# Two attention layers: the forget-attention groups placed between projections, and x loaded after the modulation blocks

## The chip, the cores and the metric

One core of one Trainium2 chip runs one program. The metric is the device time of that program in microseconds (us), the median of several runs. TensorE (PE) multiplies, VectorE (DVE) and ScalarE (ACT) work on what it leaves in the eight PSUM banks, GpSimd (POOL) does a little, and SyncE (SP) issues the DMA transfers that bring the weights.

## What is computed

A block of 256 tokens of width 1024 goes through two "hybrid" attention layers, then through two mixer layers, a dense SwiGLU and a mixture of experts. Only the attention layers are touched. One of them, cut down:

```python
shift, scale, gate = split(c @ w_ada + b_ada, 3)          # modulation, one row
u = x * (1 + scale) + shift
h = split_cols(u @ w_in)                                  # all projections
o_dsa = dsa_mixer(rope(dq), rope(dk), dv, rope(iq), rope(ik), iw)   # top-64 keys of an indexer
o_fox = fox_mixer(fq, fk, fv, log_sigmoid(f + b_f))       # forget attention, 6 heads, no rope
kc, vc = nsa_compress(h.kc, ...), nsa_compress(h.vc, ...) # silu(blocks @ w1) @ w2
o_nsa = g0*cmp(nq, kc, vc) + g1*slc(rope(nq), rope(ks), vs) + g2*win(rope(nq), rope(kw), vw)
y = (concat(o_dsa, o_fox, o_nsa) * silu(h.gate)) @ w_out
x = layer_norm(alpha * x + (1 + gate) * y)
```

Everything is 32-bit floating point.

## The kernel before

The kernel is written engine by engine: each engine has its own instruction list in program order, and the lists meet only at semaphores. `plan_first` gives every result that TensorE leaves (a "job", such as `nq01` or `S3`) one of eight PSUM banks and a turn in it. `take` makes TensorE wait until the bank is free, `filled` makes a reader wait until it is full, `copied` waits until a job's readers are done. So the order of the work is the order in which the lists are written by hand.

Weights come as "parts" of up to 2 MB through a ring of five slots; the list `loads` sets their order, and a slot is refilled when the last job of `LAST_USE` that reads it is complete. `W_IN_PARTS` cuts `w_in` into these parts. Until the first answer of TensorE is there, SyncE issues the four parts `ada0` to `ada3` of the modulation, with x between `ada1` and `ada2`, and then `idx_q`.

At the start TensorE makes the four modulation rows (`ada_row`, `ada_column`; VectorE sums four of the eight slices of each) and turns x (`turn_x`: 16 transposes into the banks `xT0` to `xT3`). VectorE (`xT0`, `xT2`) and ScalarE (`xT1`, `xT3`) scale and shift these into `uT`. Each of the four jobs holds two of the eight slices `k` that a projection sums over. The first projection, `iq`, waits for all four.

One layer then goes on TensorE in this order: index, DSA and fox projections with the eight `index_scores` between them; the NSA projections `nq01`, `nq2`, `kcvc`, `ks`, `vsw` (values), `kwg`; the compression (`ch`: 32 matmuls with 30 columns, line 979; `ckv`); then 20 attention groups (`GROUPS`): five "fox" (n = 0 to 4), two "cmp", five "win", five "slc", three "dsa". `rotate` makes the rotated copy that VectorE's `rope` needs, `ada_gate` the broadcast of the output gate from a sum that VectorE makes in the slots of `ada4` and `ada5` (`ada_sum`, eight steps each). A group is a chain over three engines:

- TensorE `scores(n)` (line 1035), VectorE `row_max(n)` (line 2265), ScalarE exponentials (line 1684),
- TensorE `transposes(n)` (line 1078), VectorE `copy_pT(n)` (line 2282),
- TensorE `outputs(n)` (line 1099), VectorE `mixed(n)` (line 2311).

The group loop runs them staggered: `scores(n)`, `transposes(n - 1)`, `outputs(n - 2)`. The projection of the output gate (1024 columns) is cut into eight `gate_part` pieces (line 991, about 3.6 us each at full clock) and strewn between the groups by `GATE_PART_AT`; ScalarE copies them out by `GATE_COPY_AT`, and VectorE's top-64 search (`select`, 16 steps) is strewn by `SELECT_AT`. `scores(0)` waits for everything the groups need, `ckv` and all ropes among it, although a fox group needs only fox projections.

Of the kernel before, what the change touches and what calls it, by code (L numbers as in the profile page):

```python
# [8 lines left out]
P = 128  # L9
D = 1024  # L10
T = 256
NT = T // P
KD = D // P
# [24 lines left out]
for _n, _w in _names:  # L38
# [5 lines left out]
              ("nsa_q", "nsa_q"), ("nsa_kc", "nsa_ks"), ("nsa_vs", "nsa_g")]  # L44
# [175 lines left out]
def plan_first(jobs, l):  # L220
# [34 lines left out]
    add("ckv", 3, 2)  # L255
    for k in range(NG + 2):
        if k < NG:
            add(f"S{k}", [0, 1, 7][k % 3])
        if 1 <= k <= NG:
            add(f"T{k - 1}", [2, 3][(k - 1) % 2])  # L260
        if k >= 2:
            add(f"O{k - 2}", [4, 5][(k - 2) % 2])
# [82 lines left out]
def build(nc, A, out_dram):  # L345
# [35 lines left out]
    for l in range(DEPTH):  # L381
        for a, b in W_IN_PARTS:
# [6 lines left out]
            if a == "nsa_kc":  # L389
                add_load((l, "cmp_w1"), 2 * CMP_LEN // 2, HD, A["cmp_w1"][l].rearrange("v (j p) m -> p (v j) m", p=P))  # L390
# [20 lines left out]
    with ctx:  # L411
# [68 lines left out]
        relu, rope_t1 = p_sb, pT  # L480
# [169 lines left out]
        def _(sp):  # L650
# [21 lines left out]
            for n, (name, k, width, src) in enumerate(loads):  # L672
# [7 lines left out]
                if name == (0, "ada1"):  # L680
                    sp.dma_start(x[:, :, :], A["x"][0].rearrange("(i p) d -> p i d", p=P)).then_inc(S("x_loaded"), 16)
# [67 lines left out]
        def _(pe):  # L749
# [103 lines left out]
            for q in range(4):  # L853
                if q == 2:
                    turn_x()
# [3 lines left out]
            ada_column(3)  # L859
            for l in range(DEPTH):  # L860
                first, second = slice(0, P), slice(P, T)
                if l == 0:
                    for m in range(4):
                        copied(pe, jobs[0, f"xT{m}"])
                    feats(l, "iq", ("idx_q", 0, P), ("idx_q", P, P))
# [85 lines left out]
                feats(l, "nq01", ("nsa_q", 0, P), ("nsa_q", P, P))  # L951
                ada_gate(0)
                feats(l, "nq2", ("nsa_q", 2 * P, P))
                feats(l, "kcvc", ("nsa_kc", 0, P), ("nsa_vc", 0, P))
                rotate(l, "nq01")
                feats(l, "ks", ("nsa_ks", 0, P))
                rotate(l, "nq2")
                j = jobs[l, "vsw"]
                b = take(pe, j)
                for i in range(NT):  # L960
                    for m, name in enumerate(("nsa_vs", "nsa_vw")):
                        last = tok(b, l, "nsa_vs", at(name), P, i, (2 * i + m) * P)
                done(last, j)
                ada_gate(1)
                j = jobs[l, "kwg"]
                b = take(pe, j)
                feat(b, l, "nsa_kw", 0, P, 0)
                for i in range(NT):
                    last = tok(b, l, "nsa_vs", at("nsa_g"), 18, i, T + 18 * i)
                done(last, j)  # L970
                rotate(l, "ks")

                j = jobs[l, "ch"]
                b = take(pe, j)
                w1 = weights(pe, (l, "cmp_w1"))
                copied(pe, jobs[l, "kcvc"])
                for v in range(2):
                    for t in range(CMP_LEN // 2):
                        last = mm(b[0:HD, 30 * v:30 * v + 30], w1[:, CMP_LEN // 2 * v + t, :], blk[:, v, t, :, :],
                                  start=(t == 0), stop=(t == CMP_LEN // 2 - 1))  # L980
                done(last, j)
                rotate(l, "kw")
# [1756 lines left out]
```

## Time and profile before

| | us |
|---|---|
| median of 3 runs | 2196.99 (2193.92 to 2197.11) |
| the profiled execution | 2193.05 |
| its span in the profile | 2191.0 |
| TensorE busy in it | 2113.2 (96%) |
| VectorE busy | 1504.8 (69%) |
| ScalarE busy | 1003.5 (46%) |

The span is what the records of the profile cover; the 2 us around it are start and end of the program. In the records a matmul on 32-bit data shows as two records, and its end is modelled, so "busy" does not mean full speed. The first 560 us or so of the span are the two attention layers, layer 0 up to about 305 us.

### The profile page before, as it was taken

To read this page: it belongs to the slowest core of one execution; us is meant where nothing else is said; L and a number is where in the kernel's file an instruction comes from. 1 tells how busy PE (TensorE), PEld (TensorE's weight loads), DVE (VectorE), ACT (ScalarE), POOL (GpSimd) and SP (SyncE) were. 2 spreads that over 40 slices of the span, in tenths; PEclk is the share of its full clock that TensorE was granted. 3 is DMA by queue.
4 is the path that set the end of the run, shared out by engine and by line. 5 is a ranking of instruction groups with operands and counts; after the bars stand their busy time and mean duration, and the time that the engine had idled before them with its cause. 6 is when DMAs were issued, how large, how long until landed. Compare 5 with 4: busy or idle time off the path is not lost.

```text
span 2191.0 us, 27918 instructions
## 1 busy us (share of the span) xinstructions
PE 2113.2 (96%) x10564; PEld 1676.5 (77%) x10564; DVE 1504.8 (69%) x1822; ACT 1003.5 (46%) x1074; POOL 52.4 (2%) x56
## 2 busy tenths in 40 slices
PE   7999999999998899999988999999999999999996
PEld 3786666765887599888757888888888888888885
DVE  4454433544398645438858888888898888889886
ACT  1111312122131434313235776777676776777674
POOL 0000000000002000000300000000000000000000
PEclk9997999889999999999998999999999999999998
DMA  9752133611531255453117999999899999999890
GB/s 352 272 186 96 43 125 116 222 39 39 177 99 51 83 174 192 166 183 117 39 56 295 395 374 350 345 352 373 321 376 330 367 347 350 370 326 377 322 354 20
DMA packets 238693, 502.18 MB, mean 229 GB/s; under 512 B 11258, under 2 KB 53010, under 8 KB 238610
## 3 DMA queue, kind: packets, MB, share of 16 engines
q1 hardware_dynamic: 238610, 501.03, 63.9%
q8 instruction: 57, 0.93, 0.2%
q14 instruction: 26, 0.21, 0.0%
HBM read 499.96 MB, written 1.05 MB: 229 GB/s over the span
## 4 chain that ended last, share of the span: by engine, by line
PE 89%; DVE 7%; ACT 2%; issue 2%; DMA 0%; SPq 0%; DVEq 0%; ACTq 0%
PE bank L1469 12%; PE bank L1452 9%; PE bank L1454 9%; PE bank L1453 9%; PE bank L760 6%; PE bank L1162 6%; PE bank L1035 3%; PE bank L991 3%; PE bank L768 3%; PE bank L1132 3%; PE bank L1399 2%; PE bank L1138 2%; PE bank L1369 2%; PE bank L1370 2%; PE bank L1368 2%; PE bank L1334 2%
## 5 line engine op out<-in xcount | busy, mean ns | idle before, releaser
L2560 DVE TENSOR_TENSOR ring_r<-ring,his 128x2048 fp32r<-128x2048 f32 x240 | 549.2, 2291 | 83.5 <-ACT his L1565 83.4
L1565 ACT ACTIVATE his<-ring 128x2048 fp32r<-128x2048 f32 x240 | 460.1, 1918 | 131.1 <-PE bank L1454 77.7
L1452 PE MATMUL bank<-his,xe_hi 128*128 128x512 f32 x896 | 356.0, 397 | 0.2 <-DVE ring_r L2560 0.2
L1454 PE MATMUL bank<-his,xe_lo 128*128 128x512 f32 x896 | 349.4, 390 | 0.0
L1453 PE MATMUL bank<-ring_r,xe_hi 128*128 128x512 f32 x704 | 274.0, 389 | 0.0
L2560 DVE TENSOR_TENSOR more_raw_r<-more_raw,his 128x2048 fp32r<-128x2048 f32 x96 | 219.8, 2291 | 32.1 <-ACT his L1565 32.0
L1565 ACT ACTIVATE his<-more_raw 128x2048 fp32r<-128x2048 f32 x96 | 184.1, 1918 | 57.4 <-PE bank L1469 32.0
L1452 PEld LDWEIGHTS bank<-his,xe_hi 128*128 128x128 f32 x896 | 168.3, 188 | 36.1 <-issue 1.7
L1454 PEld LDWEIGHTS bank<-his,xe_lo 128*128 128x128 f32 x896 | 168.2, 188 | 35.8
L1453 PEld LDWEIGHTS bank<-ring_r,xe_hi 128*128 128x128 f32 x704 | 132.3, 188 | 28.3 <-issue 1.7
L760 PE MATMUL bank<-uT,ring 128*128 128x256 f32 (+4 forms) x704 | 149.9, 372 | 2.7 <-DVE uT L2125 2.7
L1162 PE MATMUL bank<-uT,ring 128*128 128x256 f32 (+1 forms) x768 | 149.9, 357 | 0.0
L760 PEld LDWEIGHTS bank<-uT,ring 128*128 128x128 f32 (+3 forms) x704 | 119.2, 185 | 34.2 <-issue 11.7
L1469 PE MATMUL bank<-his,he_hi 128*128 128x512 f32 x448 | 142.3, 399 | 1.9 <-DVE he_lo L2648 1.9
L1162 PEld LDWEIGHTS bank<-uT,ring 128*128 128x128 f32 x768 | 131.2, 199 | 15.5 <-issue 0.5
L1469 PE MATMUL bank<-his,he_lo 128*128 128x512 f32 x448 | 138.5, 390 | 0.0
L2384 DVE SCALAR_TENSOR_TENSOR cacc<-hpad,cvec,cacc 128x256 f32<-128x256 f32 x240 | 109.6, 529 | 0.1
L1368 PE MATMUL bank<-uT_r,ff_hi 128*128 128x256 f32 (+1 forms) x384 | 108.6, 283 | 0.0
L1370 PE MATMUL bank<-uT_r,ring_r 128*128 128x256 f32 (+1 forms) x384 | 108.2, 282 | 0.0
L1369 PE MATMUL bank<-u_lo,ff_hi 128*128 128x256 f32 (+1 forms) x384 | 108.2, 282 | 0.0
L2081 DVE TENSOR_TENSOR ring_r<-ring,ff_hi 128x2048 fp32r<-128x2048 f32 (+1 forms) x34 | 74.2, 2226 | 49.4 <-ACT ff_hi L1565 49.4
L1469 PEld LDWEIGHTS bank<-his,he_hi 128*128 128x128 f32 x448 | 83.8, 189 | 22.1 <-issue 3.4
(425 smaller groups left out, 3067.5 us busy)
## 6 DMA issues: line engine op xcount, KB each, us to landing
ring<-in_moe_w_gate_dram SPq DMA_DIRECT2D x96, 1024.0 KB, 5.2
ring<-in_moe_w_up_dram SPq DMA_DIRECT2D x80, 1024.0 KB, 5.4
ring<-in_moe_w_down_dram SPq DMA_DIRECT2D x64, 1024.0 KB, 4.9
more_raw<-in_moe_w_down_dram SPq DMA_DIRECT2D x48, 1024.0 KB, 5.0
ring<-in_w_in_dram SPq DMA_DIRECT2D x16, 2048.0 KB, 9.4
more_raw<-in_moe_w_up_dram SPq DMA_DIRECT2D x32, 1024.0 KB, 5.3
ring<-in_w_ada_dram SPq DMA_DIRECT2D x12, 2048.0 KB, 9.3
ring<-in_w_out_dram SPq DMA_DIRECT2D x8, 2048.0 KB, 9.4
```

Source lines behind the costliest of these rows:

```text
L760: last = mm(b[0:n, to + tokens.start:to + tokens.stop], w[:, k, a:a + n], uT[:, k, tokens], start=(k == 0), stop=(k == KD - 1))
L1162: last = mm(b[:, f * T + tokens.start:f * T + tokens.stop], w[:, k, a:a + P], uT[:, k, tokens], start=(k == 0), stop=(k == KD - 1))
L1368: mm(o, hi[:, k, a], u_hi[:, k, tokens], start=(k == 0), stop=False)
L1369: mm(o, hi[:, k, a], u_lo[:, k, tokens], start=False, stop=False)
L1370: last = mm(o, lo[:, k, a], u_hi[:, k, tokens], start=False, stop=(k == KD - 1))
L1452: mm(bank[b][:, :], xe_hi[:, k, :], hi[:, kk, :], start=(k == 0), stop=False)
L1453: mm(bank[b][:, :], xe_hi[:, k, :], lo[:, kk, :], start=False, stop=False)
L1454: last = mm(bank[b][:, :], xe_lo[:, k, :], hi[:, kk, :], start=False, stop=(k == KD - 1))
L1469: last = mm(bank[6 + c][:, :], a[:, k, :], w[:, kk, 512 * c:512 * c + 512], start=(q == 0 and k == 0 and a is he_hi and w is hi), stop=(q ...
L1565: return go(out, in_, ACT.Copy, scale=scale)
L2384: ins = stt(cacc[:, f, :], src, w, cacc[:, f, :], ALU.mult, ALU.add)
L2560: tt(piece_lo(s), piece_raw(s), piece_hi(s).bitcast(fp32), ALU.subtract).then_inc(S("lo_ready"), 1)
```

## The change

It moves the five fox groups out of the group loop and to an earlier place: TensorE now alternates half a projection with one group's scores, the transposes of the group before and the outputs of the one before that. To do so it loads the part `nsa_kc` ahead of `nsa_q`, projects `kc`/`vc` first, gives the fox groups banks of their own (0/7, 2, 4), cuts the compression and the value projection into halves that alternate, and moves the remaining `gate_part` pieces within a loop that now starts at group 5. `scores(0)` waits for fox data only; the waits for `ckv` and for the ropes stand ahead of groups 5 and 7. VectorE's and ScalarE's lists follow this order; the sums for the output gate are cut into pieces between the groups. `rope`'s first product now goes to a half of `sg` and not to `pT`, which the fox groups use at that time. At the start, x is loaded behind `ada3`, turned after the last modulation column, and the first half of `iq` waits for the `xT` jobs one by one, two slices each.

```diff
-              ("nsa_q", "nsa_q"), ("nsa_kc", "nsa_ks"), ("nsa_vs", "nsa_g")]
+              ("nsa_kc", "nsa_ks"), ("nsa_q", "nsa_q"), ("nsa_vs", "nsa_g")]
...
-GATE_PART_AT = {2: 1, 4: 2, 7: 3, 9: 4, 12: 5, 14: 6, 17: 7}
-GATE_COPY_AT = {4: 0, 9: 1, 14: 2}
-SELECT_AT = {1: 10, 2: 11, 3: 12, 4: 13, 5: 14, 6: 15}
+NFOX = 5
+GATE_PART_AT = {5: 1, 7: 2, 8: 3, 10: 4, 12: 5, 14: 6, 16: 7}
+GATE_COPY_AT = {7: 0, 10: 1, 14: 2}
+SELECT_AT = {5: 10, 6: 11, 7: 12, 8: 13, 9: 14, 10: 15}
...
-    add("nq01", 6); add("gb0", 1); add("nq2", 2); add("kcvc", 3)
-    add("rot_nq01", 4); add("ks", 5); add("rot_nq2", 6)
-    add("vsw", 2); add("gb1", 1); add("kwg", 7); add("rot_ks", 4); add("ch", 3); add("rot_kw", 5)
+    for k in range(NFOX):
+        add(f"S{k}", [0, 7][k % 2]); add(f"T{k}", 2); add(f"O{k}", 4)
+    add("kcvc", 3); add("nq01", 6); add("nq2", 5); add("gb0", 1); add("rot_nq01", 6); add("ks", 5); add("rot_nq2", 1)
+    add("ch", 3); add("vsw", 6); add("gb1", 5); add("rot_ks", 6); add("kwg", 1); add("ckv", 3, 2); add("rot_kw", 5)
...
-        relu, rope_t1 = p_sb, pT
+        relu, rope_t1 = p_sb, sg[:, 0, :].rearrange("p (a t) -> p a t", a=2)
...
-                if name == (0, "ada1"):
+                if name == (0, "ada3"):
                     sp.dma_start(x[:, :, :], A["x"][0].rearrange("(i p) d -> p i d", p=P)).then_inc(S("x_loaded"), 16)
...
             for q in range(4):
-                if q == 2:
-                    turn_x()
                 ada_row(q)
                 if q:
                     ada_column(q - 1)
             ada_column(3)
+            turn_x()
...
-                    for m in range(4):
-                        copied(pe, jobs[0, f"xT{m}"])
-                    feats(l, "iq", ("idx_q", 0, P), ("idx_q", P, P))
...
+                    for k in range(KD):
+                        if k % 2 == 0:
+                            copied(pe, jobs[0, f"xT{k // 2}"])
+                        mm(b[:, 0:T], w[:, k, a:a + P], uT[:, k, :], start=(k == 0), stop=(k == KD - 1))
+                    done(feat(b, 0, "idx_q", P, P, T), j)
...
-                        copied(pe, jobs[l, "ckv"])
+                    if n == NFOX:
+                        for need in ("nq01", "nq2", "ckv"):
+                            copied(pe, jobs[l, need])
+                    if kind == "win" and i == 0 and heads[0] == 0:
                         copied(pe, jobs[l, "vsw"])
                         copied(pe, jobs[l, "dkv"])
                         pe.wait_ge(S("rope_done"), NR * (l + 1))
...
+                project(b, "nsa_kc", 0, 0)
+                scores(0)
+                done(project(b, "nsa_vc", 0, T), j)
+                scores(1)
+                transposes(0)
...
+                project(b, "nsa_q", 0, 0)
+                scores(2)
+                transposes(1)
+                outputs(0)
+                done(project(b, "nsa_q", P, T), j)
+                scores(3)
+                transposes(2)
+                outputs(1)
+                feats(l, "nq2", ("nsa_q", 2 * P, P))
+                scores(4)
+                transposes(3)
+                outputs(2)
+                ada_gate(0)
+                rotate(l, "nq01")
+                feats(l, "ks", ("nsa_ks", 0, P))
+                transposes(4)
+                outputs(3)
+                rotate(l, "nq2")
+                copied(pe, jobs[l, "kcvc"])
+                compress(0)
+                values(0)
+                outputs(4)
+                done(compress(1), jobs[l, "ch"])
+                done(values(1), jobs[l, "vsw"])
+                ada_gate(1)
+                rotate(l, "ks")
...
+                gate_part(0)
+                rotate(l, "kw")
+
+                for n in range(NFOX, NG + 2):
```

VectorE's new list for the same stretch:

```diff
-                ada_sum(l, 4)
-                ada_sum(l, 5)
-                for step in range(4):
-                    select(step)
...
+                ada_steps(4, 0, 1, 2, 3)
+                row_max(0)
+                ada_steps(4, 4, 5, 6, 7)
+                row_max(1)
+                copy_pT(0)
...
+                row_max(2)
+                copy_pT(1)
+                mixed(0)
+                ada_steps(5, 0, 1)
+                row_max(3)
+                copy_pT(2)
+                mixed(1)
+                ada_steps(5, 2, 3)
+                row_max(4)
+                copy_pT(3)
+                mixed(2)
...
+                rope(l, "nq01")
+                copy_pT(4)
+                mixed(3)
```

How the change moves instructions, at three places. First TensorE at the start of the program. Here `x` marks the transposes, `mix` the modulation columns. Before:

```order
L811 MATMUL bank<-const,mix 128x1 x4
L849 MATMUL bank<-const,x 128x128 x16
L801 MATMUL bank<-ring,vecs 1x512 x4
L803 MATMUL bank<-ring,const 1x512
L811 MATMUL bank<-const,mix 128x1 x4
L801 MATMUL bank<-ring,vecs 1x512 x4
L803 MATMUL bank<-ring,const 1x512
L811 MATMUL bank<-const,mix 128x1 x8
L760 MATMUL bank<-uT,ring 128x256 x16
```

With the change:

```order
L807 MATMUL bank<-const,mix 128x1 x4
L797 MATMUL bank<-ring,vecs 1x512 x4
L799 MATMUL bank<-ring,const 1x512
L807 MATMUL bank<-const,mix 128x1 x4
L797 MATMUL bank<-ring,vecs 1x512 x4
L799 MATMUL bank<-ring,const 1x512
L807 MATMUL bank<-const,mix 128x1 x8
L845 MATMUL bank<-const,x 128x128 x16
L865 MATMUL bank<-uT,ring 128x256 x8
L756 MATMUL bank<-uT,ring 128x256 x8
```

The 16 transposes of x stand behind the last modulation column, and the first 8 matmuls of `iq` are issued from a line of their own, between which the four waits stand.

Second, TensorE in layer 0 after the last index scores. Line 949 is `ada_gate`; `fk,fq` are fox scores, `blk` is the compression. Before:

```order
L760 MATMUL bank<-uT,ring 128x256 x16
L949 MATMUL bank<-ring,const 128x512
L760 MATMUL bank<-uT,ring 128x256 x24
L788 MATMUL bank<-raw_nq,const 128x512
L760 MATMUL bank<-uT,ring 128x256 x8
L788 MATMUL bank<-raw_nq,const 128x256
L768 MATMUL bank<-ring,uT 128x128 x32
L949 MATMUL bank<-ring,const 128x512
L760 MATMUL bank<-uT,ring 128x256 x8
L768 MATMUL bank<-ring,uT 128x18 x16
L788 MATMUL bank<-raw_ks,const 128x256
L979 MATMUL bank<-blk,ring 64x30 x32
```

With the change:

```order
L756 MATMUL bank<-uT,ring 128x256 x8
L988 MATMUL bank<-ff_r,pairs_r 128x128 x3
L988 MATMUL bank<-fk,fq 128x128 x2
L988 MATMUL bank<-causal_r,ident_r 128x384
L988 MATMUL bank<-fk,fq 128x128
L756 MATMUL bank<-uT,ring 128x256 x8
L988 MATMUL bank<-ff_r,pairs_r 128x128 x3
L988 MATMUL bank<-fk,fq 128x128
L988 MATMUL bank<-causal_r,ident_r 128x384
L988 MATMUL bank<-fk,fq 128x128 x2
L1031 MATMUL bank<-const,p_sb 128x128 x3
L756 MATMUL bank<-uT,ring 128x256 x8
```

Scores and transposes of the fox groups (lines 988 and 1031 of the changed kernel) stand between pieces of 8 matmuls, and from the third piece on the outputs too; before, the projections ran together, with `ada_gate` as the second thing.

Third, VectorE at the same place. `ring<-ring,vecs` are the steps of the sums for the output gate, `TENSOR_REDUCE stat` is `row_max`. Before:

```order
L2099 TENSOR_SCALAR ring<-ring,vecs 128x512
L2101 SCALAR_TENSOR_TENSOR ring<-ring,vecs 128x512 x7
L2099 TENSOR_SCALAR ring<-ring,vecs 128x512
L2101 SCALAR_TENSOR_TENSOR ring<-ring,vecs 128x512 x7
L2191 TENSOR_TENSOR isc<-isc,const 128x128
L2192 MAX m<-isc 128x8
L2193 MATCH_REPLACE isw<-m,isc 128x128
L2192 MAX m<-isw 128x8
```

With the change:

```order
L2142 TENSOR_SCALAR ring<-ring,vecs 128x512
L2144 SCALAR_TENSOR_TENSOR ring<-ring,vecs 128x512 x3
L2256 TENSOR_REDUCE stat<-bank 128x3
L2144 SCALAR_TENSOR_TENSOR ring<-ring,vecs 128x512 x4
L2256 TENSOR_REDUCE stat<-bank 128x3
L2273 COPY pT<-bank 128x384
L2325 TENSOR_TENSOR blk<-bank,pe_sb 64x8x15 x16
L2256 TENSOR_REDUCE stat<-bank 128x2
L2273 COPY pT<-bank 128x384
L2281 RECIPROCAL stat<-stat 128x3
L2302 TENSOR_TENSOR mix<-bank,stat 128x192
```

The two sums of eight steps no longer stand ahead of everything else; the first `row_max` comes after four steps of the first sum, and the rest is spread.

## Rows read from the trace of the kernel before

**Rows 1.** The page: busy time of each engine, share of the span, instructions

```profile
PE 2113.2 (96%) x10564; PEld 1676.5 (77%) x10564; DVE 1504.8 (69%) x1822; ACT 1003.5 (46%) x1074; POOL 52.4 (2%) x56
```

**Rows 2.** PE's waits, 0 to 650 us: line, awaited; us in total, times, longest

```profile
PE bank L949 <- issue: 5.4, 2, 2.7
...
PE bank L1035 <- DVE vblk L2255: 3.2, 2, 1.6
```

**Rows 3.** Chain that ended last, start of the program: start us, us, engine and line, records

```profile
22.19 1.90 PE bank L849 x16
...
35.15 1.03 PE bank L811 x8
...
38.86 12.14 PE bank L760 x48
```

**Rows 4.** VectorE (DVE) in order of time at the start: start us, us, operation

```profile
15.84 0.48 DVE L2099 TENSOR_SCALAR ring<-ring,vecs 128x512 f32<-128x512 f32 x1 [2.49 <-DMA ring<-in_w_ada_dram]
...
23.83 0.48 DVE L2099 TENSOR_SCALAR ring<-ring,vecs 128x512 f32<-128x512 f32 x1 [1.44 <-DMA ring<-in_w_ada_dram]
...
36.60 1.90 DVE L2125 TENSOR_SCALAR uT<-bank,adac 128x256 f32<-128x256 f32 x4 [0.24 <-DVE adac L2093]
```

**Rows 5.** Stretches, layer 0: busy PE, PEld, DVE, ACT, POOL; then granted clock, DMA share, GB/s

```profile
38.70:41.50 2.80, 2.64 (x6) 2.19 (x7) 0.61 (x2) 0.00 (x0) 0.00 (x0) 0.50 1.05 380
55.60:58.60 3.00, 3.00 (x9) 2.37 (x8) 2.60 (x3) 0.00 (x0) 0.57 (x1) 0.50 0.86 270
127.50:130.70 3.20, 3.20 (x10) 2.51 (x9) 3.06 (x5) 0.00 (x0) 0.00 (x0) 0.53 0.71 188
157.90:171.20 13.30, 13.30 (x81) 10.96 (x81) 4.97 (x13) 2.08 (x4) 0.98 (x1) 0.50 0.88 303
178.60:188.30 9.70, 9.61 (x20) 4.91 (x20) 2.63 (x6) 2.96 (x15) 0.00 (x0) 0.50 0.00 1
205.80:212.70 6.90, 6.90 (x20) 4.62 (x20) 3.31 (x12) 1.44 (x7) 0.00 (x0) 0.52 0.00 1
223.70:231.40 7.70, 7.70 (x46) 5.56 (x44) 5.87 (x17) 2.04 (x8) 0.00 (x0) 1.00 0.01 2
```

**Rows 6.** The same columns, layer 1

```profile
320.40:330.00 9.60, 9.60 (x64) 7.35 (x64) 1.38 (x2) 1.03 (x3) 1.98 (x2) 1.00 0.63 220
383.60:386.70 3.10, 3.10 (x7) 1.78 (x7) 2.96 (x4) 0.00 (x0) 0.00 (x0) 0.53 0.12 17
417.60:427.70 10.10, 10.10 (x57) 7.59 (x56) 4.88 (x15) 0.51 (x3) 0.90 (x1) 0.51 0.78 282
434.60:444.70 10.10, 9.66 (x17) 4.67 (x18) 2.58 (x6) 2.48 (x12) 0.00 (x0) 0.51 0.07 25
458.40:471.60 13.20, 13.20 (x45) 10.26 (x44) 5.61 (x20) 1.72 (x8) 0.00 (x0) 0.50 0.00 0
```

**Rows 7.** Chain that ended last, both layers: start us, us, engine and line, records

```profile
51.01 3.67 PE bank L768 x32
...
155.43 4.37 PE bank L768 x32
...
160.84 6.96 PE bank L979 x64
...
183.64 6.08 PE bank L991 x8
...
195.47 3.63 PE bank L991 x8
...
316.73 3.67 PE bank L768 x32
```

**Rows 8.** DMA issues from 127 to 143 us: KB each, us to landing

```profile
ring<-in_w_in_dram SPq DMA_DIRECT2D x1, 1608.0 KB, 7.1
```

**Rows 9.** VectorE: one stretch (columns as above), then one group of instructions

```profile
119.70:175.40 55.70, 51.84 (x282) 42.87 (x280) 32.95 (x86) 4.43 (x10) 3.76 (x4) 0.85 0.62 206
...
L2265 DVE TENSOR_REDUCE stat<-bank 128x2 f32<-128x512 f32 (+1 forms) x5 | 3.2, 638 | 6.2 <-PE bank L1035 6.2
```

More of the change, by code:

```diff
@@ L949, in ada_gate @@
                     done(mm(b[:, :], C("ones"), w[:, 0, :], start=True, stop=True), j)
[L951 to L982, printed above, removed]
-                def gate_part(part):
-                    c, i, half = part // 4, part // 2 % 2, part % 2
-                    j = jobs[l, f"gt{c}{i}"]
-                    b = take(pe, j)
-                    w = weights(pe, (l, f"gate{c}"))
-                    for k in range(half * (KD // 2), (half + 1) * (KD // 2)):
-                        last = mm(b[:, :], uT[:, k, i * P:(i + 1) * P], w[:, k, :], start=(k == 0), stop=(k == KD - 1))
-                    if half:
-                        done(last, j)
@@ L1101, in outputs, with gate_part @@
                     done(last, j)
-                for n in range(NG + 2):
+                def gate_part(part):
+                    c, i, half = part // 4, part // 2 % 2, part % 2
+                    j = jobs[l, f"gt{c}{i}"]
+                    b = take(pe, j)
+                    w = weights(pe, (l, f"gate{c}"))
+                    for k in range(half * (KD // 2), (half + 1) * (KD // 2)):
+                        last = mm(b[:, :], uT[:, k, i * P:(i + 1) * P], w[:, k, :], start=(k == 0), stop=(k == KD - 1))
+                    if half:
+                        done(last, j)
@@ new lines, in project, with compress @@
+                def project(b, name, c0, to):
+                    return feat(b, l, name, c0, P, to)
+                def compress(v):
+                    w1 = weights(pe, (l, "cmp_w1"))
+                    b = take(pe, jobs[l, "ch"])
+                    for t in range(CMP_LEN // 2):
+                        last = mm(b[0:HD, 30 * v:30 * v + 30], w1[:, CMP_LEN // 2 * v + t, :], blk[:, v, t, :, :],
+                                  start=(t == 0), stop=(t == CMP_LEN // 2 - 1))
+                    return last
@@ new lines, in values @@
+                def values(i):
+                    b = take(pe, jobs[l, "vsw"])
+                    for m, name in enumerate(("nsa_vs", "nsa_vw")):
+                        last = tok(b, l, "nsa_vs", at(name), P, i, (2 * i + m) * P)
+                    return last
+                j = jobs[l, "kcvc"]
+                b = take(pe, j)
+                project(b, "nsa_kc", 0, 0)
[3 more added lines that the diff above has]
+                transposes(0)
@@ new lines, in _ @@
+                b = take(pe, j)
+                feat(b, l, "nsa_kw", 0, P, 0)
+                for i in range(NT):
+                    last = tok(b, l, "nsa_vs", at("nsa_g"), 18, i, T + 18 * i)
+                done(last, j)
+                j = jobs[l, "ckv"]
+                b = take(pe, j)
+                pe.wait_ge(S("ch_ready"), l + 1)
+                mm(b[0:HD, 0:30], w2[:, l, 0, :], ch[:, 2, 0, :], start=True, stop=True)
+                done(mm(b[0:NHC, HD:2 * HD], chrep[:, :, :, :], w2[:, l, 1, :], start=True, stop=True), j)
```

168 lines of the change are left out of this document (89 added, 79 removed).

## The prediction

> **What bounds the kernel now.** The page comes first: TensorE is busy in 2113.2 us, 96% of the span of 2191.0 [rows 1], so time can only be won where TensorE waits, or where it runs at half its clock while it is called busy. VectorE, at 69%, is no bound on the whole. The change touches the start and, in each of the two attention layers, the stretch from the last index scores to the last attention group; everything behind 560 us stays as it is and only moves.
>
> Next, TensorE's waits in the first 650 us [rows 2] and the start of the chain that ended last [rows 3]. Three waits belong to the change. In each layer `ada_gate(0)` (line 949) stands still for 2.7 us. The view calls the releaser "issue", but in program order it is the sum of `ada4`, which VectorE makes at that moment. In each layer `scores(0)` (line 1035) stands 1.6 us until `vblk` is written. Once, at the start, the last column ends at 36.2 and the first projection (line 760) begins at 38.86 [rows 3]: 2.7 us for `uT`. Together 5.4 + 3.2 + 2.7 = 11.3 us.
>
> Then the granted clock, which costs more. In layer 0 the clock is at half (1.2 GHz of 2.4) in four stretches of the touched region, 3.2, 13.3, 9.7 and 6.9 us long from 127.5 on [rows 5], and in layer 1 in four stretches of 3.1, 10.1, 10.1 and 13.2 us from 383.6 on [rows 6]. They sum to 69.6 us. What TensorE did before each: in two it had stood still for `ada_gate` (127.5, 383.6); in two it had come through the `scores(0)` wait and two bare groups (178.6, 434.6); in four it had run without a gap, but on narrow matmuls: the 18 columns of `kwg` and the 30 of the compression (157.9, 417.6), and the outputs and the 15-column scores around the "cmp" groups (205.8, 458.4). The same `gate_part` takes 6.08 us in such a stretch and 3.63 outside it [rows 7].
>
> **The change, part by part.**
>
> *Start.* x (1024 KB) leaves its place between `ada1` and `ada2`. From `ada1` to `ada2`, x and the 2048 KB of `ada2` took 23.83 - 15.84 = 7.99 us [rows 4], so x is worth 2.7 us and `ada2` and `ada3` arrive that much earlier. Against that, 16 transposes that lay in the gap before `ada2` now stand behind the last column. The path of the end: `ada_row(2)` follows the transposes today, which begin at 22.19 and take 1.90; it can now start at 22.2, which brings the last column from 36.2 to about 34.4, and the transposes then end at 36.3 [rows 3]. `uT` needs 1.90 us on VectorE after the last column today [rows 4], but its first slice pair needs half of that and runs beside the transposes. So `iq` starts at about 36.3 and not at 38.9: **-2.5**. SyncE passes x behind two parts, and only the transposes read it. The clock was at half for 2.8 us behind that wait [rows 5]; if the wait goes, up to 1.4 more comes back. The bounds are 1.5 and 3.9; I take 2.5, since the columns and transposes ahead are as thin as before.
>
> The page "TensorE: Matmul & The Clock Gate" of the Trainium skill, section "Part 4: PE-mode transpose", says that transposes do not count as work for the clock. By it `iq` would begin at the lower clock as today and the start brings its 2.5 only; no row here tells transposes apart.
>
> *The two waits per layer.* The sum of `ada4` is now spread over VectorE's list and complete well before `ada_gate(0)`, which stands behind group 4's scores: **-5.4**. `scores(0)` needs fox projections alone, which are copied when `kc` has run: **-3.2**. Do the waits come back elsewhere? `scores(5)` now waits for `ckv`, whose second reader on VectorE stands behind six search steps; TensorE has a `gate_part` (3.6 us), a rotation and, before them, `kwg` to cover it. VectorE was busy 32.95 of 55.7 us between the index scores and `scores(0)` [rows 9]. The five groups add a `row_max` of 0.64 us each [rows 9], a copy and a mix of like length, some 10 us in all, while TensorE's stretch gets about as much longer: 43 of 60 us. That holds, with 1 us for small gaps: **+1**.
>
> *The clock.* If all 69.6 us ran at full clock and all work doubled in speed, half would go: 34.8. The narrow matmuls do not double. The 32 records of line 768 take 3.67 us at full clock and 4.37 partly at half [rows 7], only 16% less. I count the 12.3 us of compression at half (6.96 in layer 0 [rows 7], 5.3 in layer 1) at 16% and not at 50%: 4.2 less, 30.6 left. Bounds 30.6 and 34.8; I take **-31**, near the end that the narrow row measures.
>
> *What stays of it.* The new order has three thin stretches per layer: transposes, outputs and first half of the compression (some 5 us), `outputs(4)` and the second half (4), the 18 columns of `kwg` with `ckv` (4). Between them stand at least 3.4 us of wide matmuls, and the "cmp" groups now have a `gate_part` on either side. Rows for such a stretch alone: 3.67 us of line 768 at 51.0 was followed by a half-clock stretch of 3.0 us; the same at 316.7 was followed by none [rows 5, 6, 7]. So six places, of which I let four fall, at half of some 3.2 us: **+6.4**. Bounds 0 and, if each fell for 9.7 us as at 178.6, 29. That fox groups between wide matmuls keep the clock is seen at 223.7: 7.7 us of scores, transposes and outputs at clock 1.00 [rows 5].
>
> *Costs nothing.* `nsa_kc` and `nsa_q` are equally large and swap places. `nsa_vs` still waits for the slot of `ada4`, so for `ada_gate(0)`, which comes later now; it took 7.1 us to land [rows 8]. TensorE then has `ks` (3.6), half the compression (3.5) and 2 to 3 us of small work: 2 us to spare. The weights behind it have more. The table load of ScalarE for the exponentials comes into the chain of group 0, under `vc`. Moving `gate_part` leaves three "dsa" groups without one instead of two: below 0.5.
>
> *Sum.* -2.5 - 5.4 - 3.2 + 1 - 31 + 6.4 = -34.7. On the profiled execution's 2193.05 that is 2158.4. Its own time lies 3.9 below the median of 2196.99 and near the lowest run, 2193.92; I put the median of the changed kernel slightly above the sum: **2160 us**.
>
> **The rivals.**
>
> *A: only the drops behind waits go.* The clock fell four times behind narrow work without any gap, and that work is all still there. If it falls as long as before, only the halves of 3.2 + 9.7 + 3.1 + 10.1 = 26.1 us come back, 13. With 2.5 + 5.4 + 3.2 that is 24: 2169, as a median 2171. For it: PE is 13.30 of 13.30 us busy in the longest of them [rows 5]. Against it: the narrow work is now broken up. The page named above, section "HAM oscillation — how this bites in real kernels", tells of the clock falling after gaps in which the engine idles, and asks to keep gaps short. By that alone the narrow stretches would not matter and their new order would bring nothing, which is this rival; the rows at 157.9 and 458.4, half clock without a gap, speak against the rule as a whole account. Chance 0.18.
>
> *B: the clock gives nothing.* As many half-clock microseconds appear elsewhere. Then -11.1 + 1: 2183. Chance 0.05.
>
> *C: a weight comes late.* `nsa_vs` misses `values(0)`, by up to 3 us per layer if other transfers share the queue, with a clock drop of 1.6 behind it: +9, 2169. Chance 0.07.
>
> *D: slower.* VectorE's list, strict in order, now holds `row_max` and the copies between sums, gate bias, ropes, search steps and the 16 additions for the compression. If TensorE stands before a group as it stands today before `ada_gate`, that is 2.7 us and 1.6 of clock, 4.3 a group, ten groups: +43, net +8, 2201. It decides from the point at which VectorE is late for eight of the ten. Its load of 43 in 60 us speaks against it. Chance 0.02.
>
> *E: it does not do what it says.* If new waits and thin stretches eat the whole gain, the time stays within 0.2%, 4.4 us, which is about what a measurement here tells from no change. Chance 0.02.
>
> **How the numbers follow.** The forecast keeps 0.66; its own range runs from full effect (3.9 + 8.6 + 34.8 = 47, 2146) to six drops and the smaller bounds (about 29, 2165). To hold eight in ten I go up over A to 2175 and leave B and D out: 2147 to 2175. Faster: all but D and E, 0.96; same 0.02; slower 0.02.
>
> **What would show it.** Right: no wait at the lines of `ada_gate`, `scores(0)` or `scores(5)` above 0.5 us; `iq` starting near 36.3; half-clock stretches in the two layers summing to 10 to 25 us, not 70, none around groups 5 to 7; each layer from its last index scores to its last group some 16 us shorter; the time behind 560 us unchanged in length. Wrong: half-clock stretches of 10 us at the compression (A), TensorE waiting for the slot of `nsa_vs` (C) or for `row_max` and `pT` (D), or a start of `iq` at 38 or later.

## The result and the profile after

| | before | changed |
|---|---|---|
| median, us | 2195.45 of 4 runs (2191.62 to 2197.11) | 2161.18 of 4 runs (2160.86 to 2165.70) |
| profiled execution, us | 2193.05 | 2165.70 |
| its span, us | 2191.0 | 2163.9 |
| at half clock in the first 600 us | 85.4 | 44.4 |

The ratio is 0.9854, 95% interval 0.9839 to 0.9869: faster, by 34.3 us in the medians. The profiled execution of the changed kernel is its slowest of four, so the two traces are only 27.1 us of span apart. The last line of the table is summed over slices of 1 us from the granted clock of each; so are all such sums below.

The page of the changed kernel, where [rows 1] had 2113.2 us of TensorE:

```profile
PE 2097.1 (97%) x10564; PEld 1664.2 (77%) x10564; DVE 1505.0 (70%) x1822; ACT 1004.5 (46%) x1074; POOL 51.2 (2%) x56
```

TensorE has the same 10564 matmul records and is busy for 16.1 us less. What it is spared while busy is clock, and the other 11 us of the span are waits. TensorE's waits of the changed kernel, 0 to 560 us (line, awaited; us in total, times, longest):

```profile
PE bank L797 <- DMA ring<-in_w_ada_dram: 5.9, 1, 5.9
PE bank L788 <- DMA const<-in_const_dram: 4.7, 1, 4.7
PE bank L1153 <- DVE mix L2392: 3.4, 2, 1.7
PE bank L1031 <- ACT p_sb L1692: 1.2, 2, 0.6
PE bank L807 <- DVE adac L2136: 0.3, 1, 0.3
```

Neither `ada_gate` nor the scores stand here any more [rows 2]. The first, second and last line are of the start, and the `mix` line stands behind the last group. Nothing is new.

Where the rest came from is read from the chain that ended last, by four marks: the first projection behind the last index scores, and the output projection behind the last group, in each layer. The kernel before (start us, us, line, records; line 1132 is the output projection, 1165 in the changed kernel):

```profile
116.30 7.10 PE bank L760 x32
...
271.67 21.76 PE bank L1132 x48
...
373.44 7.10 PE bank L760 x32
...
530.02 20.60 PE bank L1132 x48
```

The changed kernel, with its start and the rows that the prediction spoke of:

```profile
34.53 3.11 PE bank L845 x16
37.64 3.92 PE bank L865 x16
41.55 7.02 PE bank L756 x32
48.58 3.68 PE bank L764 x32
...
113.87 3.65 PE bank L756 x16
...
151.77 1.98 PE bank L1076 x32
153.75 3.77 PE bank L764 x32
...
173.94 5.86 PE bank L1063 x8
...
189.84 6.44 PE bank L1063 x8
...
257.28 20.60 PE bank L1165 x48
...
359.53 3.65 PE bank L756 x16
...
500.66 21.66 PE bank L1165 x48
```

Subtracting the marks, stretch by stretch, changed against before (us):

| stretch | before | changed | difference | predicted |
|---|---|---|---|---|
| start to the last index scores | 116.30 | 113.87 | -2.4 | -2.5 |
| layer 0 from there to its output projection | 155.37 | 143.41 | -12.0 | about -16 |
| to the last index scores of layer 1 | 101.77 | 102.25 | +0.5 | 0 |
| layer 1 to its output projection | 156.58 | 141.13 | -15.4 | about -16 |
| all behind | 1660.98 | 1663.24 | +2.3 | 0 |
| sum | | | -27.1 | -34.7 |

A second profile of the same changed kernel (`e11_changed_again`, below; marks 114.83, 252.22, 354.46 and 495.07, span 2155.9) gives -1.5, -18.0, +0.5, -16.0 and -0.2, together -35.1. One execution lies on either side of the prediction, and what differs between them is above all where the clock fell.

The stretches of the changed kernel at half clock, columns as in [rows 5]:

```profile
34.90:38.60 3.70, 3.70 (x18) 3.50 (x17) 1.99 (x4) 1.95 (x4) 1.35 (x6) 0.54 1.05 388
52.10:55.50 3.40, 3.40 (x10) 2.77 (x10) 3.26 (x5) 0.44 (x2) 0.91 (x1) 0.50 1.05 366
...
171.80:178.60 6.80, 6.80 (x17) 3.94 (x17) 2.77 (x7) 0.85 (x4) 0.72 (x1) 0.52 1.05 383
189.00:195.80 6.80, 6.80 (x11) 3.13 (x11) 1.20 (x4) 1.36 (x7) 0.00 (x0) 0.52 0.00 0
253.90:257.00 3.10, 3.10 (x15) 3.10 (x16) 1.03 (x1) 1.49 (x3) 0.00 (x0) 0.52 0.00 0
304.90:308.30 3.40, 3.40 (x18) 3.40 (x18) 0.00 (x0) 0.44 (x2) 0.72 (x1) 0.53 0.51 170
417.50:424.20 6.70, 6.70 (x16) 3.88 (x16) 2.73 (x7) 0.86 (x4) 0.72 (x1) 0.50 1.05 387
434.40:437.80 3.40, 3.40 (x6) 1.67 (x6) 1.46 (x5) 1.62 (x7) 0.00 (x0) 0.50 0.00 0
499.50:502.80 3.30, 3.30 (x9) 1.97 (x8) 0.00 (x0) 2.56 (x4) 0.00 (x0) 0.52 0.00 0
```

In the touched regions four are left, 6.8 + 6.8 + 6.7 + 3.4 = 23.7 us where [rows 5, 6] had 69.6. In each of them TensorE is busy without a gap. Two begin in the 18-column matmuls of `kwg` (171.8, 417.5), and two right behind the 15-column scores of the second "cmp" group, in the scores of group 7 (189.0, 434.4). The fox groups and the compression ahead of them run at full clock. The stretch at 253.9 stood at 270 to 274 before, behind the mark and not ahead of it: it puts about 1 us of layer 0's gain into the third line of the table. The ones at 304.9 and 499.5 had no counterpart: part of the gain is given back at narrow places that the change does not touch.

### The profile page after: what moved, and what is told of

Same layout as the page of the kernel before. It is cut to its first block, busy times and chain, and to the rows that moved or that the text cites. A ratio compares the mean times of both kernels' runs of the same rounds, so it can differ in the third digit from the quotient of the medians.

```text
span 2163.9 us, 27922 instructions
## 1 busy us (share of the span) xinstructions
PE 2097.1 (97%) x10564; PEld 1664.2 (77%) x10564; DVE 1505.0 (70%) x1822; ACT 1004.5 (46%) x1074; POOL 51.2 (2%) x56
## 4 chain that ended last, share of the span: by engine, by line
PE 89%; DVE 7%; ACT 2%; issue 1%; DMA 0%; SPq 0%; DVEq 0%; ACTq 0%
PE bank L1502 12%; PE bank L1485 9%; PE bank L1487 9%; PE bank L1486 9%; PE bank L756 6%; PE bank L1195 6%; PE bank L1063 3%; PE bank L988 3%; PE bank L764 3%; PE bank L1165 3%; PE bank L1432 2%; PE bank L1171 2%; PE bank L1403 2%; PE bank L1402 2%; PE bank L1401 2%; PE bank L1367 2%
## 5 line engine op out<-in xcount | busy, mean ns | idle before, releaser
L756 PEld LDWEIGHTS bank<-uT,ring 128*128 128x128 f32 (+3 forms) x688 | 114.4, 184 | 27.4 <-issue 6.5
L1598 ACT ACTIVATE ff_hi<-ring 128x2048 fp32r<-128x2048 f32 (+1 forms) x34 | 61.4, 1858 | 85.1 <-PE bank L1403 57.0
```

The lines of the kernel that those rows point to most:

```text
L756: last = mm(b[0:n, to + tokens.start:to + tokens.stop], w[:, k, a:a + n], uT[:, k, tokens], start=(k == 0), stop=(k == KD - 1))
L1598: return go(out, in_, ACT.Copy, scale=scale)
```

## The experiments

All runs in one table; the ratio is to the kernel before in the same batch, "half clock" the sum over the first 600 us of the profiled execution.

| kernel | median, us (runs) | ratio (95%) | half clock, us |
|---|---|---|---|
| `e1_start_only` | 2190.28 (11) | 0.9975 (0.9962 to 0.9987) | 88.8 |
| `e2_groups_only` | 2168.88 (4) | 0.9872 (0.9857 to 0.9887) | 51.2 |
| `e3_gate_wait` | 2193.53 (11) | 0.9988 (0.9979 to 0.9997) | 85.3 |
| `e34_waits_only` | 2185.64 (5) | 0.9955 (0.9941 to 0.9969) | 78.5 |
| `e34b_waits_clean` | 2181.49 (5) | 0.9936 (0.9922 to 0.9950) | 85.3 |
| `e9_waits_and_narrow` | 2178.06 (5) | 0.9919 (0.9905 to 0.9932) | 61.4 |
| `e5_compress_whole` | 2163.84 (4) | 0.9854 (0.9839 to 0.9869) | 44.3 |
| `e11_changed_again` | 2162.83 (4) | 0.9855 (0.9840 to 0.9870) | 34.1 |
| `e7_gate_at_6` | 2161.25 (5) | 0.9844 (0.9831 to 0.9858) | 37.5 |
| `e6_kwg_split` | 2160.45 (5) | 0.9837 (0.9824 to 0.9850) | 23.9 |
| `e67_fill_last_two` | 2155.11 (5) | 0.9818 (0.9805 to 0.9831) | 20.5 |
| `e10_fill_more` | 2151.91 (5) | 0.9798 (0.9785 to 0.9812) | 17.0 |

### The two parts of the change apart

`e1_start_only` is the kernel before with the start alone, `e2_groups_only` the changed kernel with the old start:

```diff
-                if name == (0, "ada1"):
+                if name == (0, "ada3"):
...
-                if q == 2:
-                    turn_x()
                 ada_row(q)
...
             ada_column(3)
+            turn_x()
```

> The kernel before with the start of the change alone: x loaded behind ada3, turned behind the last modulation column, and the first half of iq waiting for the four xT jobs one by one. Theory of the prediction: one wait of 2.7 us goes and iq ends 2.4 us earlier, as in the changed kernel (48.58 instead of 51.01), with nothing of it given back later: 2193 on a kernel before of 2195.5. Rival, the start is lost again because the weights that follow are bound by DMA: 2195.5, with TensorE waiting for a weight between 50 and 120 us. Rival, the lower clock stays longer behind the transposes: above 2195.5.

> The changed kernel with the start of the kernel before: the fox groups between the projections alone. Theory of the prediction: both attention regions keep what they won, 12.6 us in layer 0 and 16.1 in layer 1, so 2161.2 + 2.4 = 2163.6. Rival, the parts depend on each other through the moments at which the clock is decided: then it is off from 2163.6 by more than 3 us either way.

Measured: -5.3 us and -26.7 us against a median before of 2195.58 in their batch. The start alone ends the last index scores 2.45 us earlier, as in the whole change; its median is better than that by 2.9, and its runs spread from 2183.81 to 2193.59. The groups alone fell 5.3 us short of what was expected; it came out as the rival said, more than 3 us off. In their profile two stretches at half clock near the start (37 to 45 and 54 to 62) are 6.8 us each by the slices, where the whole change has 3.7 and 3.4. The parts add to -32.0 where the whole has -34.3: near, but a part's effect hangs on where the clock falls with it.

### Only the waits taken away

`e3_gate_wait` moves the standing `ada_gate(0)` behind two projections, `e34_waits_only` also lets `scores(0)` go without `ckv`, and `e34b_waits_clean` has the same two edits with the gate behind one projection only. The fox groups stay where they were. The last one:

```diff
-                ada_gate(0)
                 feats(l, "nq2", ("nsa_q", 2 * P, P))
+                ada_gate(0)
                 feats(l, "kcvc", ("nsa_kc", 0, P), ("nsa_vc", 0, P))
...
                         pe.wait_ge(S("fox_ready"), l + 1)
+                    if n == 5:
                         copied(pe, jobs[l, "ckv"])
```

> The kernel before with one line moved: ada_gate(0) behind kcvc on TensorE, when VectorE's sum is complete. No group is moved. Theory that the clock falls behind a wait: the wait of 2.7 us in each layer goes and with it the half-clock stretch of 3.2 us behind it, 2 x (2.7 + 1.6) = 8.6, so 2187. Rival, only the wait goes: 5.4, so 2190. Rival, the clock falls at that point anyway or later: 2190 with a half-clock stretch of about 3 us elsewhere before 157 us.

> The kernel before with that move and with scores(0) freed of its wait for ckv (the wait stands ahead of the cmp groups); all groups stay behind the projections. Theory that the interleaving is needed because narrow matmuls alone let the clock fall: the waits go (5.4 + 3.2) and the 3.2 us half-clock stretches behind ada_gate, but the stretches at the compression, the first groups and the cmp groups stay: 2185 to 2188, with about 55 to 63 us at half clock in the two layers. Rival A (drops come from waits alone): the stretches at 178.6 and 434.6 go too, 9.9 us more: 2176 to 2178.

> The kernel before with ada_gate(0) one projection later (behind nq2 and not behind kcvc, so that the weights that wait for its slot are asked for at the old time) and scores(0) freed of its wait for ckv. No weight should come late this time. Theory that narrow stretches hold the clock down by themselves: waits 5.4 + 3.2 gone, half-clock stretches at 127 and 383 gone, the others stay with some 60 us: 2195.5 - 12 = 2183.5. Rival A, the stretches behind scores(0) go too: 2174 to 2178. Rival, the half-clock time only moves: 2187.

`e3_gate_wait` hardly gained (-2.1). Its chain, layer 0, tells why:

```profile
134.33 0.87 PE bank L949 x2
135.21 0.02 issue
135.22 7.17 DMA ring<-in_w_in_dram
142.39 0.14 issue
142.53 7.38 PE bank L768 x64
```

`ada_gate` (line 949) is the last reader of the slot of `ada4`; the transfer of `nsa_vs` starts when it is done, takes 7.17 us, and the values (line 768) stand 2.9 us for it here and 5.5 us in the two layers together, for the 5.4 us removed. The wait came back as another: this is rival C's mechanism, shown, though not in the changed kernel. There `ada_gate(0)` ends at 145.7, the transfer takes 6.8 us and the values begin at 153.75: about 1 us is to spare, where the prediction had 2. `e34_waits_only` has the same late transfer (5.2 us of waits for it in the two layers) and loses only the wait at `scores(0)`: -9.9 us, and 2185.64 lies in the 2185 to 2188 that was expected.

With the gate one projection earlier the new wait is gone too. TensorE's waits of `e34b_waits_clean`, 100 to 560 us, whole:

```profile
PE bank L1121 <- DVE mix L2327: 3.4, 2, 1.7
PE bank L1079 <- ACT p_sb L1685: 2.4, 4, 0.6
```

and its stretches at half clock in the touched regions:

```profile
158.10:171.70 13.60, 13.60 (x75) 9.92 (x74) 7.48 (x21) 1.60 (x3) 0.98 (x1) 0.52 0.96 327
178.50:185.30 6.80, 6.80 (x10) 2.77 (x10) 0.69 (x1) 1.02 (x4) 0.00 (x0) 0.54 0.00 0
199.00:212.60 13.60, 13.60 (x45) 10.13 (x45) 5.34 (x18) 1.72 (x8) 0.00 (x0) 0.52 0.00 1
410.20:423.80 13.60, 13.60 (x76) 10.32 (x77) 6.45 (x17) 2.09 (x4) 0.97 (x1) 0.51 0.75 264
430.60:437.40 6.80, 6.80 (x10) 2.97 (x10) 1.41 (x4) 1.02 (x4) 0.00 (x0) 0.51 0.12 45
454.50:461.30 6.80, 6.80 (x19) 4.67 (x20) 3.37 (x12) 1.44 (x7) 0.00 (x0) 0.51 0.00 0
```

TensorE is busy in 61.2 of 61.2 us by these records, whose ends are modelled, and the clock is at half all the same. The stretches at 127.5 and 383.6, right behind the standing gate, are gone [rows 5, 6], and those behind `scores(0)` are shorter, but others have grown: in the touched regions 61.2 us are left of 69.6, in the first 600 us 85.3 of 85.4. So most of the half clock does not hang on the gaps. By the four marks (119.56, 270.24, 372.49, 520.53) the two layers are 13.2 us shorter, 8.6 of it the waits, and the start is 3.3 longer, where two stretches of 6.8 us by the slices stand for two of 3.4. In the medians the edit is worth 15.0 us, a little more than expected: not much less than half of what the whole change gains comes without moving a group.

### Narrow work broken up without moving the groups

`e9_waits_and_narrow` adds to that the halves of the compression between halves of the values, and `gate_part` 3 one group earlier:

```diff
+                values(0)
+                copied(pe, jobs[l, "kcvc"])
+                compress(0)
+                done(values(1), j)
+                done(compress(1), jobs[l, "ch"])
                 ada_gate(1)
...
-GATE_PART_AT = {2: 1, 4: 2, 7: 3, 9: 4, 12: 5, 14: 6, 17: 7}
+GATE_PART_AT = {2: 1, 4: 2, 6: 3, 9: 4, 12: 5, 14: 6, 17: 7}
```

> The same, and the narrow work broken up where it stands, with the fox groups left behind the projections: the two halves of the compression between the two halves of the value projection, and a gate_part between the two cmp groups (n = 6 instead of 7). Theory that what the change gained is the clock in narrow stretches and not the place of the groups: most of the half-clock time at 158 and 205 (layer 0) and 417 and 458 (layer 1) goes, 20 to 30 of 60 us, 10 to 15 us of time: 2169 to 2174. Rival, the interleaving of the groups with wide projections is what keeps the clock: 2180 to 2184, near the run without this.

Its compression, a piece of the view by stretches, and one of its waits:

```profile
144.00:155.00 11.00, 11.00 (x118) 10.18 (x118) 4.29 (x19) 0.60 (x1) 0.00 (x0) 1.00 0.01 1
```

```profile
PE bank L788 <- ACT sgate L1665: 3.1, 2, 1.5
```

The clock holds through the compression, and 24 us of half clock go, worth up to 12; the median moved by 3.4 only. By the marks (119.36, 266.37, 368.68, 514.97) the two layers are 5.4 us shorter than in `e34b_waits_clean`: the new wait of 3.1 us, for ScalarE behind a table load of its own, eats into the gain, and 2.6 us come back behind the last group. Stretches around the bare groups stay (174 to 182, 198 to 205, 423 to 431, 447 to 455). It did not reach what was expected. Against the changed kernel some 15 us are missing. The start is 2.4 to 5.3 of them and the new wait 3.1; that the rest needs the groups among the projections is argued, no run shows it by itself.

`e5_compress_whole` asks the same of the changed kernel, with the two halves of the compression parted by `outputs(4)` alone:

```diff
                 compress(0)
-                values(0)
                 outputs(4)
                 done(compress(1), jobs[l, "ch"])
+                values(0)
```

> The changed kernel with the two halves of the compression back to back (with outputs(4) between them) and the value halves behind them: a thin stretch of about 7 us in each layer. Theory: the clock falls there in both layers, the value projection runs part of its time at half, +2 to +4 us per layer: 2165 to 2169. Rival, the clock does not care for one such stretch: 2161.

```profile
150.00:165.00 15.00, 15.00 (x152) 13.82 (x152) 8.03 (x27) 0.89 (x3) 0.73 (x1) 1.00 1.02 362
```

The clock is 1.00 and the ratio that of the changed kernel to four digits, so my expectation of one more drop fell. Putting the values between the two halves earns nothing here. In the kernel before, the compression stood right behind `kwg`, and in layer 0 the clock fell at 157.9, in the 18-column matmuls of `kwg` and before the compression began at 160.84 [rows 5, 7]. So it may be enough that the compression stands away from them; no run tests that alone.

### The places that are left

`e6_kwg_split` parts the two halves of `kwg`'s 18-column matmuls with the wide half of that job; `e7_gate_at_6` moves two `gate_part` pieces to groups 6 and 7; `e67_fill_last_two` does both:

```diff
-                feat(b, l, "nsa_kw", 0, P, 0)
-                for i in range(NT):
-                    last = tok(b, l, "nsa_vs", at("nsa_g"), 18, i, T + 18 * i)
-                done(last, j)
+                tok(b, l, "nsa_vs", at("nsa_g"), 18, 0, T)
+                feat(b, l, "nsa_kw", 0, P, 0)
+                done(tok(b, l, "nsa_vs", at("nsa_g"), 18, 1, T + 18), j)
...
-GATE_PART_AT = {5: 1, 7: 2, 8: 3, 10: 4, 12: 5, 14: 6, 16: 7}
-GATE_COPY_AT = {7: 0, 10: 1, 14: 2}
+GATE_PART_AT = {5: 1, 6: 2, 7: 3, 10: 4, 12: 5, 14: 6, 16: 7}
+GATE_COPY_AT = {6: 0, 10: 1, 14: 2}
```

> The changed kernel with its two remaining half-clock places filled: the 18-column matmuls of kwg split around its wide half, and gate_part 2 between the two cmp groups (n = 6 and 7 instead of 7 and 8). Theory: the half-clock stretches at 171 and 188 (layer 0) and 417 and 434 (layer 1), 23.8 us together, mostly go, 6 to 12 us of time: 2150 to 2156. Rival, they move to the next thin place: 2159 to 2163.

> The changed kernel with the 18-column matmuls of kwg split around its wide half, and nothing else. Theory: the half-clock stretches at 171 (layer 0) and 417 (layer 1), 6.8 us each, go, and those at the cmp groups stay: half of what both edits together brought, 2157 to 2159. Rival, it alone brings all (the later stretches followed from the earlier): 2155. Rival, nothing without the other: 2161.

> The changed kernel with gate_part 2 at group 6 and 3 at group 7 (before 7 and 8), and nothing else. Theory: the stretches at 188 (6.8 us) and 434 (3.4 us) go, those at 171 and 417 stay: 2158 to 2160, less up to 1 us given to a later wait for the copy of the gate. Rivals as for the other half: 2155 or 2161.

`e6_kwg_split`: no fall at `kwg`, one behind the "cmp" groups in layer 0 and none in layer 1.

```profile
165.00:175.00 10.00, 10.00 (x59) 8.36 (x60) 9.10 (x29) 0.85 (x4) 0.73 (x1) 1.00 0.94 327
186.00:189.40 3.40, 3.40 (x6) 1.55 (x6) 1.04 (x3) 1.16 (x7) 0.00 (x0) 0.55 0.00 0
```

`e7_gate_at_6`: the other way round.

```profile
172.00:179.00 7.00, 7.00 (x19) 3.70 (x19) 2.99 (x8) 0.85 (x4) 0.72 (x1) 0.56 1.05 385
185.00:200.00 15.00, 15.00 (x56) 7.98 (x55) 5.07 (x17) 2.03 (x8) 0.00 (x0) 1.00 0.11 28
```

`e67_fill_last_two`: full clock through both places in both layers.

```profile
172.00:195.00 23.00, 23.00 (x85) 12.61 (x85) 9.46 (x29) 3.18 (x13) 0.73 (x1) 1.00 0.43 144
411.00:440.00 29.00, 28.52 (x106) 15.73 (x107) 15.09 (x46) 5.38 (x22) 0.72 (x1) 1.00 0.57 204
```

Each edit cleared its own place, with no wait removed (the `gate_part` edit adds 1.0 us of waits for `sg`) and no matmul less. A single profile would not prove it, since the falls move from one execution to the next. All profiles together do, for `kwg`: in the eleven that keep its 18-column matmuls in one piece, the kernel before among them, the clock falls while they run or within 2.2 us of their end, in both layers, 22 times of 22, and TensorE stands still for nothing in the 4 us ahead of them. In the three that part them (this one, `e6_kwg_split` and `e10_fill_more`) it does so 0 times of 6. Behind the second "cmp" group the count is weaker: 8 times of 10 in the five profiles of the changed order without the `gate_part` edit, one of the two exceptions in the unedited kernel itself, and 0 of 6 with it. So the same columns in another order decide whether the clock falls. In the medians neither edit alone can be told from the changed kernel (the intervals overlap), and each lies nearer to the 2161 of no effect than to what was expected; both together can (0.9818 against 0.9855), and 2155.11 is within what was expected. `e6_kwg_split` fell into runs near 2156 and near 2161, and `e7_gate_at_6` had a new stretch at 493 to 501: while a thin place is left, a cleared one is not yet a gain.

`e10_fill_more` does both, puts the copy of a `gate_part` at group 9 to spare TensorE a 1.0 us wait for `sg`, and parts the 8-column matmuls of `ikw` in the same way:

```diff
-                feat(b, l, "idx_k", 0, IDX_DIM, 0)
-                for i in range(NT):
-                    last = tok(b, l, "idx_q", at("idx_w"), IDX_HEADS, i, T + IDX_HEADS * i)
-                done(last, j)
+                tok(b, l, "idx_q", at("idx_w"), IDX_HEADS, 0, T)
+                feat(b, l, "idx_k", 0, IDX_DIM, 0)
+                done(tok(b, l, "idx_q", at("idx_w"), IDX_HEADS, 1, T + IDX_HEADS), j)
```

> The changed kernel with both edits, the copy of the second gate bank one group earlier (9 instead of 10), and the 8-column matmuls of ikw split around its wider half in both layers. Theory: the wait of 0.5 us per layer for the gate copy goes, and so do the half-clock stretches of 3.4 us at 51 and 297: 2155.1 - 1 - 3 = 2151. Rival, the first is set by the start and the second by the end of layer 0, not by ikw: 2154.

The stretches at 52 and 305 are gone, one at 246 to 251 is new, and the median of 2151.91 is the lowest of all, 44.0 us below the kernel before in its batch. Against `e67_fill_last_two` the intervals still touch. By the four marks (112.01, 248.48, 349.84, 485.48) its two layers are 18.9 and 20.9 us shorter than before, and 3.6 us are given back behind.

### The changed kernel once more

> The changed kernel once more, unedited, beside the others. Theory that the 4.7 us between its profiled run (2165.7) and its other runs (2161) is the clock at other moments of the same program behind the attention layers, and not work: median 2161 again, another profile with the same waits, and a span that follows the granted clock. Rival: 2165 is its time and the three others were low.

```profile
173.80:177.20 3.40, 3.40 (x6) 1.50 (x5) 1.78 (x4) 0.47 (x3) 0.72 (x1) 0.51 1.04 386
412.60:419.40 6.80, 6.80 (x15) 3.48 (x15) 2.58 (x6) 0.85 (x4) 0.72 (x1) 0.52 1.05 387
```

The same program, unedited, has 34.1 us at half clock here and 44.4 in the first profile, at 2157.67 and 2165.70 us. The two times differ by 8.0, and the traces account for it: up to 2140 us the slices count 104.8 us at half in the first and 92.1 in this one, 12.7 less, worth 5.5 at the 0.43 us for each that is worked out below, and TensorE's idle time is 2.3 us less. The eight runs of this program lie between 2157.67 and 2165.70.

## Why the prediction was right, point by point

Forecast 2160, range 2147 to 2175; measured 2161.18 and, again, 2162.83. The mechanism held: two waits per layer gone, and most of the half clock gone with narrow work spread out. That the number is so near is in part luck. The two profiled executions of the one program lie 5.7 above and 2.3 below 2160, the price of narrow work was right only in sum, and the half clock that stays was put too low for one of them and about right for the other.

- **Start, -2.5: right in sum, not in its steps.** The last column ended at 34.53 (predicted 34.4). The transposes then took 3.11 us and not 1.90, because the clock was at half from 34.9, so `iq` began at 37.64 and not at 36.3. But then only 1.0 us of `iq` itself ran at half, where 2.8 had [rows 5], and the first 48 records took 3.92 + 7.02 = 10.94 us against 12.14 [rows 3]. The last index scores end 2.4 earlier. By the page's rule that transposes do not count as work for the clock (the Trainium skill, "TensorE: Matmul & The Clock Gate", "Part 4: PE-mode transpose") `iq` would begin at the lower clock, and it did; the one-column matmuls ahead of the transposes are just as thin, so the runs do not tell which of the two it was.
- **Waits, -5.4 - 3.2: right.** Both are gone, and nothing replaces them on any engine; VectorE was busy 36.4 of 56 us from 119 to 175, where 43 of 60 was predicted. The +1 for new gaps did not show: the waits for the exponentials rather shrank, 1.8 to 1.2.
- **Clock, -31: right in size, wrong in its reason.** The step "the narrow matmuls do not double", priced at 16% from line 768, is wrong. The 64 records of the compression took 6.96 us at half [rows 7] and 2 x 1.98 = 3.96 at full clock, 43% less. The two rows of line 768 were different jobs and the slower one was only partly at half. With 43% on 12.3 us and a half on all else the term would have been -34.0. The runs bear out -31 all the same. In `e67_fill_last_two` no half clock is left in the two layers; by its marks (113.44, 249.64, 351.89, 488.08) they are 39.6 us shorter than before. TensorE's waits there are 8.2 less, so 31.4 are the clock, for 72.9 us at half before (between the marks, by slices): 0.43 us for each. The changed kernel's two profiles give 18.2 for 44.1 and 24.8 for 59.3, 0.41 and 0.42. Where the missing part between 0.43 and 0.5 goes, beyond the narrow matmuls' 43%, no run shows.
- **What stays, +6.4: half of what stayed in one profile, about right in the other, and in part at other places.** Six places were counted and four let fall, at half of 3.2. The clock fell at four in the first profile and held at both halves of the compression; it fell at `kwg` as named (twice), but also behind group 6, where the prediction said none. It had counted a `gate_part` on either side of the "cmp" groups, but `GATE_PART_AT` puts none between group 6 and the scores of group 7, where the fall is. Three of the four were twice as long as 3.2. Between the marks 28.8 us at half are left in the first profile and 13.6 in the second, worth 12 and 6. So the two layers, predicted 32.2 shorter, are 27.4 shorter in the first and 34.0 in the second.
- **Behind the two layers, 0: nearly.** +2.3 in one profile, -0.2 in the other, and +3.8 and +3.6 in `e67_fill_last_two` and `e10_fill_more`: the code there is the same, but the clock falls at other moments. Behind the last mark the slices count 70.5 us at half before, and 76.0, 74.0, 77.4 and 77.3 in these four.

Rival A, that only the drops behind waits go, is refuted. With the waits alone removed, 8.4 us of half clock went from the touched regions and none in sum (`e34b_waits_clean`), where the change takes 46; and with narrow work parted and no wait taken away, more of it went (`e67_fill_last_two`). The rule of the Trainium skill ("TensorE: Matmul & The Clock Gate", "HAM oscillation — how this bites in real kernels"), which ties the falling clock to idle gaps, is therefore not the whole account: 61.2 us at half with TensorE busy in all 61.2 speak against it, as far as the profile's busy time is a measure of idle gaps: the ends of matmuls are modelled, and gaps within narrow records would not show. Rival B is excluded by the clock sums and rival E by the ratio. C was shown as a mechanism, D never appeared: no `row_max` or `copy_pT` is waited for in the touched regions.

Open: what moving the groups gives by itself, without the waits (the medians leave some 19 of the 34 us to it and to the start); and how narrow, for how long, work has to be before the clock falls, which varied between executions of one program.

## What to carry to other kernels

When an engine is "96% busy", look at the granted clock of its busy time: here 70 us of the two layers ran at half, and ordering narrow matmuls (8 to 30 columns, small groups) between wide ones gave about as much as taking the waits away (15.0 us for the waits alone, 34.3 with both and the start, 44.0 with the order refined). Before you take such a wait away, ask which buffer the waiting instruction releases, since its transfer then starts later (`e3_gate_wait`). Expect a cleared place to be partly paid at the next thin one, and clear several before you judge.

## What was not expected of the hardware

- TensorE's clock went to half with no idle time in the profile: 13.60 of 13.60 us busy at a granted clock of 0.52, where the work was narrow. It fell each time at 32 records of 18 columns in one piece (22 of 22), and never where 16 wide ones parted them (0 of 6).
- A microsecond at half clock cost these two layers 0.41 to 0.43 us, not 0.5.
- A narrow matmul gains nearly as much from the clock as a wide one: a record of the compression (30 columns) took 109 ns at half and 62 ns at full clock.
- One program does not take one time: eight runs of the changed kernel lie 8.0 us apart, eleven of `e1_start_only` 9.8, with the clock falling at other moments in each profile. It sets the smallest effect that one run can show.
